# Gate z of the delta stage taken out of PSUM by halves during its last chunk, with the next products begun on the first half's bank, and a new order of VectorE's work at the turn

## The chip, the cores and the metric

One core of one Trainium2 chip. The metric is device microseconds of one execution. Before the change three runs gave a median of 2839.73 us (2836.88 to 2842.76).

## The reference, cut to what matters

Two transformer-like blocks on 256 tokens of width 2048, in float32. The change lies in the first mixer, a gated delta network with 32 value heads of 128:

```python
proj = h @ w_in
qkv, z, b, a = jnp.split(proj, [...], axis=-1)
qkv = jax.nn.silu(causal_depthwise_conv(qkv, conv_w))
q, k, v = ...                      # q and k scaled to length 1 per head
o = gated_delta_rule(q, k, v, g, beta)
o = o * lax.rsqrt(jnp.mean(o * o, -1, keepdims=True) + NORM_EPS)
o = (o.astype(h.dtype) * norm_w) * jax.nn.silu(z.reshape(B, S, GDN_V_HEADS, HEAD_DIM))
return o.reshape(B, S, GDN_DV) @ w_out
```

Here h is 256 x 2048 and w_in has 12352 columns. Behind this mixer come its output product, a layer norm, the feed-forward part and a second block; the change touches none of them.

## The kernel before, in words

The engines run as separate programs that meet at semaphores. Every matrix product is done in three fp32r products, high x high, high x low and low x high. A weight tile ("chunk") of 256 x 512 is loaded into `wr` (ring of 4); ScalarE copies it rounded to `wh` (`gh`, L1402 to L1406, ring of 3); GpSimd subtracts to get the rest `wl` (`low`, L594 to L598); TensorE multiplies. ScalarE may write the tile of chunk c once TensorE is through chunk c-3; GpSimd starts on it when ScalarE is through. In this document wl(n) is GpSimd's subtraction for chunk n of the next group and gh(n) ScalarE's copy for it.

The delta network is worked in 8 groups of 4 value heads (NIT = 8). A group takes 24 chunks: 8 for q and k (into PSUM tile `pg[0]`), 8 for v (`pg[1]`), 8 for z (`pg[0]` again). While the chunks of group j+1 run, the delta rule of group j is worked between them: TensorE runs one step of the generator `delta` behind nearly each chunk (`beside`, L1095 to L1110). The last step but one (rows "v1", "o1", "md1") stands ahead of chunk 23. The z chunks have tokens on the partitions: token half 0 goes to the first 512 columns of `pg[0]`, which is one PSUM bank, token half 1 to the second. In chunk 23 TensorE does the six products of half 0 first, then the six of half 1.

The **turn** is what lies between chunk 23 of one group and the first steps of the next:

- TensorE, chunk 0 of the next group (L797 to L831): waits for `s_zo` (z has left `pg[0]`), then 24 products. Behind it come step "ssq" of the next delta (L918; it waits for `s_sq1`, VectorE's squares of q and k, and for "md1", the end of VectorE's `mod_sum`, which reads the same PSUM tile), step "on" of the old one (eight transposes, L738), chunk 1, step "rows" (L926), chunk 2, step "gram" (L936; it waits for "qkn", VectorE's scaled q and k, L1948), and step "ktok", which waits for "dt" (VectorE, L1953).
- ScalarE: `gh(1)`, then the last step of the old delta: four squares with sums of the second half of the output (L1477), Ln and Exp for `rstd` (L1541, L1542), then `z_out` (L1452 to L1455: one copy of 128 x 1024 out of `pg[0]`), then `gh(2)`.
- VectorE: o1 (L2014), output times gate (L2018), `mod_sum` (a reduce out of PSUM, L2030, and a small addition, L2033), `squares` of q and k for the next group (L1913), output times `rstd` (L2025), and, once TensorE's transposes are done, `finish` (L2038). The next delta begins with four copies: L1942, and the three of `taps`, L1859, L1860 and L1861; then L1948 and L1953.
- GpSimd: wl(1), wl(2), then for the next group a product of 64 x 512 (L630), two DMA issues for the modulation weights (L591), wl(3), wl(4) and so on.

The product `mod_w` for the modulation vectors is done beside all this on VectorE (L1833, L1835). Six turns (groups 1 to 2 up to 6 to 7) have the z chunks of one group ahead of the q and k chunks of the next. The first turn has z in `pd[1]`, not in `pg[0]`. After the last group the output product (`ochunk`, L833 to L850) begins in place of chunk 0. On ScalarE and VectorE the iterations 0 to 5 are a hardware loop and iteration 6 stands behind it as straight code.

Of the kernel before, what the change touches and what calls it, by code (L numbers as in the profile page):

```python
# [17 lines left out]
ACT = mybir.ActivationFunctionType  # L18
# [8 lines left out]
NIT = NQK // 2  # L27
VH = 4
# [33 lines left out]
NCH = 24  # L62
N_GDN = NCH * (NIT + 1)
RING = 3
# [52 lines left out]
def build(nc, A, out):  # L117
    ctx = ExitStack()
    with ctx:
# [3 lines left out]
        def sem(name):  # L123
            return ctx.enter_context(nc.semaphore(name))
# [45 lines left out]
        zpend = take(VH, T)  # L170
# [167 lines left out]
        pg = [ctx.enter_context(nc.psum_tensor(f"pg{i}", [P, 1024], F32)) for i in range(2)]  # L338
        pd = [ctx.enter_context(nc.psum_tensor(f"pd{i}", [P, 1024], F32)) for i in range(2)]
# [17 lines left out]
        s_pk = sem("s_pk")  # L357
# [4 lines left out]
        s_qk = sem("s_qk")  # L362
        s_sq1 = sem("s_sq1")
        s_ot = sem("s_ot")
        s_zo = sem("s_zo")
        s_cv = sem("s_cv")
        s_acc = sem("s_acc")
# [367 lines left out]
        def _(pe):  # L735
# [30 lines left out]
            for t, n in enumerate(V_ROWS):  # L766
                dst = pd[0][:, 512 + t * P:512 + t * P + n] if t < 4 else pd[1][:, 512:512 + n]
                m = tr(dst, vstage[0:n, t, :])
# [4 lines left out]
            for kt in range(KD):  # L773
                b = kt // 4
# [4 lines left out]
                for t in range(TT):  # L779
                    m = tr((pg[0], pg[1], pd[1], pg[0])[b][:, (kt % 4) * T + t * P:(kt % 4) * T + (t + 1) * P],  # L780
                           xtok[:, t, kt * P:(kt + 1) * P])
# [13 lines left out]
            def gchunk(g, c):  # L795

                first_g = isinstance(g, int) and g == 0  # L797
                grp, kp = chunk_of(g, c)
                if c == 0 and not first_g:
                    pe.wait_ge(s_zo, g)  # L800
                    pe.wait_ge(s_cd, g * 2 - 1)
                if c == 8 and not first_g:
                    pe.wait_ge(s_cd, g * 2)
                if c == 16 and not first_g:
                    pe.wait_ge(s_cd, g * 2 + 1)
                pe.wait_ge(s_low, g * NCH + (c + 5))
                bank, first, last = pg[grp % 2], kp == 0, kp == 7
                if first_g and grp == 2:
                    bank = pd[1]
                if grp == 2:  # L810
                    for t in range(TT):
                        for k in range(2):
                            for i, (x, w) in enumerate(((0, wh), (0, wl), (1, wh))):
                                m = nc.tensor.matmul(halves(bank)[:, t, :], h_s[x][:, 2 * kp + k, t * P:(t + 1) * P],  # L814
                                                     w[c % RING][:, k, :], skip_group_check=True,
                                                     start=(first and k == 0 and i == 0),
                                                     stop=(last and k == 1 and i == 2))
                    m.then_inc(s_pk, 1)
                    return
                for n in range(4):  # L820
                    for k in range(2):
                        for i, (w, x) in enumerate(((wh, 0), (wh, 1), (wl, 0))):
                            m = nc.tensor.matmul(bank[:, n * T:(n + 1) * T], w[c % RING][:, k, n * P:(n + 1) * P],  # L823
                                                 h_s[x][:, 2 * kp + k, :], skip_group_check=True,
                                                 start=(first and k == 0 and i == 0 and n % 2 == 0),
                                                 stop=(last and k == 1 and i == 2))
                m.then_inc(s_pk, 1)

            def ochunk(c):

                if c == 0:  # L831
                    pe.wait_ge(s_zo, NIT)
                if c == 12:  # L833
                    pe.wait_ge(s_cd, NIT * 2)
                pe.wait_ge(s_low, NIT * NCH + (c + 5))
                g, kp = c // 12, c % 12
                if c == 0:
                    pe.wait_ge(s_osv, 1)
                elif 2 <= c < 12:
                    pe.wait_ge(s_os, kp // 2)  # L840
                for h in range(TT):
                    for k in range(2):
                        for i, (x, w) in enumerate(((0, wh), (0, wl), (1, wh))):
                            m = nc.tensor.matmul(halves(pg[g])[:, h, :], o_s[x][:, 2 * kp + k, h * P:(h + 1) * P],  # L844
                                                 w[c % RING][:, k, :], skip_group_check=True,
                                                 start=(kp == 0 and k == 0 and i == 0), stop=False)
                m.then_inc(s_pk, 1)
# [14 lines left out]
            for c in range(4):  # L862
                pe.wait_ge(s_h3, c + 1)
                m = gate_sums(c)
# [33 lines left out]
            for t, (row, w) in enumerate(((3, 0), (3, 1), (2, 0), (2, 1), (0, 0))):  # L898
                m = tr(pd[0][:, 512 + t * NH:512 + (t + 1) * NH], gx[0:NH, row, w * P:(w + 1) * P])
# [260 lines left out]
            for t in range(CK_FF):  # L1160
                g, k, last = out_chunk(t)
# [9 lines left out]
                if t == 4:  # L1171
                    pe.wait_ge(s_v, NIT * len(VO))
                    for i in range(2):
                        m = row_of(pd[i], 2 * KD + 8 * i)
                    m.then_inc(s_pp, 1)
                if t == 15:
# [4 lines left out]
                    for c in range(3):  # L1181
                        m = tr(pd[0][:, c * PAIRS:(c + 1) * PAIRS], araw[0:PAIRS, c, :])
                    m.then_inc(s_pp, 1)
                    for c in range(8):
                        m = tr(pd[1][:, c * P:(c + 1) * P], craw[1][:, c, :])
                    m.then_inc(s_pp, 1)
                if t == 19:
                    pe.wait_ge(s_craw[0], 128)
                    pe.wait_ge(s_ap, 2)
                    for c in range(8):  # L1190
                        m = tr(pd[0][:, c * P:(c + 1) * P], craw[0][:, c, :])
                    m.then_inc(s_pp, 1)
                if t == 38:
                    pe.wait_ge(s_vp, 1)
                    pe.wait_ge(s_ap, 4)
                    for i in range(2):
                        for c in range(8):
                            m = tr(pd[i][:, c * P:(c + 1) * P],
                                   bbar[i][:, 4 * c:4 * c + 4, :].rearrange("p a b -> p (a b)"))
# [150 lines left out]
        def _(act):  # L1350
            link, restart = chain(act, s_aa)
            a = nc.scalar.activation
# [96 lines left out]
                    a(pend[:, grp * 4 + n, :], pg[grp][:, n * T:(n + 1) * T], ACT.Copy,  # L1449
                      scale=cwc[:, 3, grp * 4 + n:grp * 4 + n + 1]).then_inc(s_cv, 1)  # L1450

            def z_out(g):  # L1452
                act.wait_ge(s_pk, g * NCH + (NCH + RING))
                a(zpend.rearrange("p a b -> p (a b)"), (pd[1] if isinstance(g, int) and g == 0 else pg[0])[:], ACT.Copy)\  # L1454
                    .then_inc(s_zo, 1)  # L1455

            def silu_qk(g):
# [7 lines left out]
                a(vT.rearrange("p a b -> p (a b)"), pend[:, 4:8, :].rearrange("p a b -> p (a b)"), ACT.Silu).then_inc(s_a, 1)  # L1465

            def silu_z(g):
                act.wait_ge(s_zo, g + 1)
                a(zt.rearrange("p a b -> p (a b)"), zpend.rearrange("p a b -> p (a b)"), ACT.Silu).then_inc(s_a, 1)

            def delta(it, more):
                bp, bv = it * len(PEO), it * len(VO)
                def PEw(name): act.wait_ge(s_pe, bp + PEO[name])
                def V(name): act.wait_ge(s_v, bv + VO[name])
                def squares(n0):
                    for n in range(n0, n0 + VH):
                        link(a(Tb[:, n, :], ob[:, n, :], ACT.Square, accum_out=ssq[:, n:n + 1]))  # L1477
                restart()
                PEw("ssq")
# [33 lines left out]
                for h in range(VH):  # L1513
                    m = a(vn0[:, h, :], pd[0][:, h * P:(h + 1) * P], ACT.Copy, scale=tkc[:, 2, h:h + 1])
# [6 lines left out]
                for h in range(VH):  # L1521
                    m = a(ob[:, VH + h, :], pd[0][:, 512 + h * P:512 + (h + 1) * P], ACT.Copy, scale=tkc[:, 4, h:h + 1])
# [5 lines left out]
                for h in range(VH):  # L1528
                    m = a(vn1[:, h, :], pd[1][:, h * P:(h + 1) * P], ACT.Copy, scale=tkc[:, 3, h:h + 1])
# [6 lines left out]
                    act.sem_inc(s_a, 1)  # L1536
                nc.scalar.preload_act_table_set("natural_log_exp_and_others")
                yield
                V("o1")
                squares(VH)  # L1540
                link(a(rstd, ssq, ACT.Ln, scale=1.0 / P, bias=cst[:, 0:1]))  # L1541
                a(rstd, rstd, ACT.Exp, scale=-0.5).then_inc(s_a, 1)  # L1542
                yield
# [11 lines left out]
            silu_qk(0)  # L1555
            gh(1, 0)
            gh(1, 1)
            z_out(0)
            gh(1, 2)
            silu_v(0)  # L1560
            nc.scalar.preload_act_table_set("natural_log_exp_and_others")
# [23 lines left out]

            def turn(j, more=None):

                z_out(j + 1)
                if more:
                    more()  # L1590
                gh(j + 2, 2)
# [197 lines left out]
        def _(dve):  # L1789
# [119 lines left out]
            def squares(it):  # L1909

                dve.wait_ge(s_qk, it + 1)
                fq = qk.rearrange("p a b -> p (a b)")
                v.tensor_tensor(sqb, fq, fq, ALU.mult).then_inc(s_sq1, 1)  # L1913
# [21 lines left out]
            def delta(it, mods):  # L1935
                bp, ba, bv = it * len(PEO), it * len(AO), it * len(VO)
                def PEw(name): dve.wait_ge(s_pe, bp + PEO[name])
                def Ac(name): dve.wait_ge(s_a, ba + AO0 + AO[name])
                def done(m): m.then_inc(s_v, 1)
# [10 lines left out]
                for c in range(TT):  # L1950
                    for h in range(VH):
                        n = c * VH + h
                        m = stt(out=dTb[:, n, :], in0=pd[0][:, n * P:(n + 1) * P], scalar=tkc[:, c, h:h + 1], in1=mneg[:],  # L1953
                                op0=ALU.subtract, op1=ALU.min)
# [4 lines left out]
                for c in range(TT):  # L1959
                    for h in range(VH):  # L1960
                        n, b = c * VH + h, c * 2 + h // 2
                        m = stt(out=lTb[:, n, :], in0=pd[1][:, b * P:(b + 1) * P], scalar=tkc[:, 2 + c, h:h + 1],
                                in1=dTb[:, n, :], op0=ALU.mult, op1=ALU.mult)
                done(m)
                dve.wait_ge(s_v, bv + VO["lt"])
                for b in range(2):
                    r = slice(64 * b, 64 * b + 64)
                    m = v.tensor_tensor(by_n(four(Uc[r])), heads(lTb[r, :, r]),
                                        m1t[r, 0:64].unsqueeze(1).unsqueeze(1).broadcast_to([64, 4, 2, 64]), ALU.mult)
# [46 lines left out]
                dve.wait_ge(s_v, bv + VO["o1"])  # L2016
                Ac("z")
                done(v.tensor_tensor(oz, ob, zt, ALU.mult))  # L2018
                PEw("md1")
                mod_sum(it, 1)  # L2020
                if mods:
                    squares(it + 1)
                dve.wait_ge(s_v, bv + VO["oz"])
                Ac("rstd")
                done(v.tensor_tensor(oz, oz, rstd.unsqueeze(2).broadcast_to([P, 8, P]), ALU.mult))  # L2025
# [295 lines left out]
            for t in range(TT):  # L2321
                for i in range(2):
                    part, cut = res[:, t, 1024 * i:1024 * (i + 1)], slice(1024 * i, 1024 * (i + 1))
# [169 lines left out]
```

## Time and profile before

| | |
|---|---|
| median of 3 runs | 2839.73 us (2836.88 to 2842.76) |
| the profiled execution's own time | 2838.75 us |
| its span, first to last instruction | 2836.8 us |
| TensorE busy | 2715.5 us (96%) |
| VectorE, ScalarE, GpSimd busy | 1948.6, 1208.2, 812.2 us |
| mean granted TensorE clock | 0.984 |

The span is 1.95 us shorter than the execution's time; that part lies around the program. All times of rows are us from the start of the span. A timeline row gives start, duration, engine, line, operation, operands and, in brackets, how long the engine had been idle and what ended it. Where a row joins several instructions the duration is that of all of them. An instruction whose start lies ahead of its predecessor's end is pipelined behind it.

### The profile page before, as it was taken

To read this page: it belongs to the slowest core of one execution; us is meant where nothing else is said; L and a number is where in the kernel's file an instruction comes from. 1 tells how busy PE (TensorE), PEld (TensorE's weight loads), DVE (VectorE), ACT (ScalarE), POOL (GpSimd) and SP (SyncE) were. 2 spreads that over 40 slices of the span, in tenths; PEclk is the share of its full clock that TensorE was granted. 3 is DMA by queue.
4 is the path that set the end of the run, shared out by engine and by line. 5 is a ranking of instruction groups with operands and counts; after the bars stand their busy time and mean duration, and the time that the engine had idled before them with its cause. 6 is when DMAs were issued, how large, how long until landed. Compare 5 with 4: busy or idle time off the path is not lost.

```text
span 2836.8 us, 48694 instructions
## 1 busy us (share of the span) xinstructions
PE 2715.5 (96%) x18902; PEld 2341.8 (83%) x18902; DVE 1948.6 (69%) x2285; ACT 1208.2 (43%) x1521; POOL 812.2 (29%) x554
## 2 busy tenths in 40 slices
PE   6999999999998999999999999969999999999998
PEld 3788988898896877888888888769999998888886
DVE  1377877787688667666666666685999899655554
ACT  2255455545545444433433333344333334543443
POOL 1066666676667510000000000000565562000000
PEclk8999999999999999999999999989999999999999
DMA  9866665675664666666666666535555555666664
GB/s 364 309 199 215 224 216 195 207 253 183 213 224 155 224 184 209 191 187 190 188 189 187 187 190 187 168 112 177 155 158 158 161 167 161 191 187 189 189 202 147
DMA packets 283912, 552.59 MB, mean 195 GB/s; under 512 B 16817, under 2 KB 54258, under 8 KB 282610
## 3 DMA queue, kind: packets, MB, share of 16 engines
q1 hardware_dynamic: 263632, 474.02, 54.3%
q0 software_dynamic: 19408, 76.06, 7.2%
q8 instruction: 122, 2.00, 0.3%
q10 hardware_dynamic: 722, 0.28, 0.0%
q14 instruction: 28, 0.23, 0.0%
HBM read 548.19 MB, written 2.10 MB: 194 GB/s over the span
## 4 chain that ended last, share of the span: by engine, by line
PE 80%; DVE 11%; ACT 4%; issue 2%; DMA 2%; DVEq 0%; POOL 0%; ACTq 0%; SPq 0%; POOLq 0%; PEld 0%
PE pg L1132 25%; PE pd L1132 17%; PE pg L823 13%; PE pg L1119 9%; PE pg L814 4%; DVE wl L2074 2%; PE pd L738 2%; PE pg L844 2%; DMA arena<-in_mod_w 1%; PE pd L987 1%; PE pd L1005 1%; DVE arena L2355 1%; DVE arena L2357 1%; DVE arena L2350 1%; ACT arena L1477 1%
## 5 line engine op out<-in xcount | busy, mean ns | idle before, releaser
L2074 DVE TENSOR_TENSOR wl<-wr,wh 128x1024 fp32r<-128x1024 f32 x616 | 773.7, 1265 | 507.7 <-ACT wh L1597 504.4
L1597 ACT ACTIVATE wh<-wr 128x1024 fp32r<-128x1024 f32 x616 | 652.7, 1060 | 997.7 <-PE pg L1132 405.4
L597 POOL TENSOR_TENSOR wl<-wr,wh 128x1024 fp32r<-128x1024 f32 x195 | 479.3, 2459 | 395.2 <-ACT wh L1406 395.0
L1406 ACT ACTIVATE wh<-wr 128x1024 fp32r<-128x1024 f32 x216 | 227.7, 1057 | 350.3 <-PE pg L823 219.9
L1119 PE MATMUL pg<-hh,wh 128*128 128x256 f32 x1280 | 366.5, 286 | 3.8 <-ACT arena L1715 2.5
L1119 PE MATMUL pg<-hl,wh 128*128 128x256 f32 x1280 | 363.0, 284 | 0.0
L1119 PE MATMUL pg<-hh,wl 128*128 128x256 f32 x1280 | 362.7, 283 | 0.0
L1132 PE MATMUL pg<-wh,hh 128*128 128x512 f32 x832 | 327.2, 393 | 0.0
L1132 PE MATMUL pg<-wl,hh 128*128 128x512 f32 x832 | 326.3, 392 | 0.0
L1132 PE MATMUL pg<-wh,hl 128*128 128x512 f32 x832 | 325.4, 391 | 0.0
L823 PE MATMUL pg<-hh,wh 128*128 128x256 f32 x1024 | 301.2, 294 | 14.8 <-ACT arena L1454 12.0
L1835 DVE SCALAR_TENSOR_TENSOR arena<-arena,condt 128x512 f32<-128x512 f32 x240 | 281.1, 1171 | 29.3 <-DMA arena<-in_mod_w 23.7
L823 PE MATMUL pg<-hl,wh 128*128 128x256 f32 x1024 | 290.2, 283 | 0.0
L823 PE MATMUL pg<-hh,wl 128*128 128x256 f32 x1024 | 290.0, 283 | 0.0
L1119 PEld LDWEIGHTS pg<-hh,wh 128*128 128x128 f32 x1280 | 246.1, 192 | 16.1 <-issue 13.4
L727 POOL COPY arena<-arena 128x256 f32 x8 | 6.4, 798 | 875.5 <-ACT arena L1715 875.5
L1119 PEld LDWEIGHTS pg<-hh,wl 128*128 128x128 f32 x1280 | 246.2, 192 | 0.0
L1119 PEld LDWEIGHTS pg<-hl,wh 128*128 128x128 f32 x1280 | 246.1, 192 | 0.0
L823 PEld LDWEIGHTS pg<-hh,wh 128*128 128x128 f32 x1024 | 196.4, 192 | 33.1 <-ACT arena L1454 14.6
L823 PEld LDWEIGHTS pg<-hl,wh 128*128 128x128 f32 x1024 | 196.8, 192 | 0.2 <-issue 0.2
L823 PEld LDWEIGHTS pg<-hh,wl 128*128 128x128 f32 x1024 | 196.7, 192 | 0.0
L1132 PEld LDWEIGHTS pg<-wh,hh 128*128 128x128 f32 x832 | 156.3, 188 | 34.9 <-issue 0.4
(392 smaller groups left out, 5033.1 us busy)
## 6 DMA issues: line engine op xcount, KB each, us to landing
wr<-in_w_in SPq DMA_DIRECT2D x224, 512.0 KB, 3.9
wr<-in_ffn_w_gu SPq DMA_DIRECT2D x176, 512.0 KB, 4.3
wr<-in_gdn_w_in SPq DMA_DIRECT2D x128, 512.0 KB, 4.0
arena<-in_mod_w POOLq DMA_DIRECT2D x64, 1024.0 KB, 7.4
wr<-in_ffn_w_down SPq DMA_DIRECT2D x88, 512.0 KB, 3.8
arena<-in_mod_w SPq DMA_DIRECT2D x32, 1024.0 KB, 12.2
wr<-in_gdn_w_in SPq DMA_DIRECT2D x128, 256.0 KB, 2.9
wr<-in_gdn_w_out SPq DMA_DIRECT2D x56, 512.0 KB, 4.7
```

Of the source, the lines that this page charges most:

```text
L597: nc.gpsimd.tensor_tensor(wl[c % RING][:], wraw[c % 4], wh[c % RING][:].bitcast(F32), ALU.subtract)\
L738: return nc.tensor.transpose(dst, src, ident[0:n, 0:n])
L814: m = nc.tensor.matmul(halves(bank)[:, t, :], h_s[x][:, 2 * kp + k, t * P:(t + 1) * P], w[c % RING][:, k, :], skip_group_check=True, start ...
L823: m = nc.tensor.matmul(bank[:, n * T:(n + 1) * T], w[c % RING][:, k, n * P:(n + 1) * P], h_s[x][:, 2 * kp + k, :], skip_group_check=True, ...
L844: m = nc.tensor.matmul(halves(pg[g])[:, h, :], o_s[x][:, 2 * kp + k, h * P:(h + 1) * P], w[c % RING][:, k, :], skip_group_check=True, star ...
L987: m = nc.tensor.matmul(block(pd[par], *crossed(s, b, n)), lTb[r, n, r], Tc[r, n, :], start=True, stop=True)
L1119: m = nc.tensor.matmul(bank[:, n * T:(n + 1) * T], w[s][:, k, n * P:(n + 1) * P], act[x][:, k0 + k, :], skip_group_check=True, start=(firs ...
L1132: m = nc.tensor.matmul(halves(bank)[:, h, :], act[x][:, k0 + k, h * P:(h + 1) * P], w[s][:, k, :], skip_group_check=True, start=(first and ...
L1406: a(wh[c % RING][:], wraw[c % 4], ACT.Copy).then_inc(s_hi, 1)
L1597: a(wh[c % 4][:], wraw[c % 4], ACT.Copy).then_inc(s_hc, 1)
L1835: m = stt(out=dst, in0=mw[t % 2][:, k, :], scalar=condt[:, kk:kk + 1], in1=dst, op0=ALU.mult, op1=ALU.add)
L2074: v.tensor_tensor(wl[c % 4][:], wraw[c % 4], wh[c % 4][:].bitcast(F32), ALU.subtract).then_inc(s_lc, 1)
```

## The change

z is taken out in two halves, each 512 columns. A new semaphore, `s_zh`, is raised by the last product of token half 0 in chunk 23; ScalarE's first half waits for it, the second half for the end of the chunk. The first half stands ahead of the four squares of the last delta step, the second between the second and the third of them. `s_zo` counts halves now. TensorE's chunk 0 waits for the first half ahead of its first 12 products and for the second half ahead of the other 12; the first chunk of the output product does the same by token halves. On VectorE `squares` of the next group stands ahead of `mod_sum` at the turn. In the first group both halves wait for the end of the chunk, one behind the other.

```diff
@@ gchunk (TensorE)
                 if c == 0 and not first_g:
-                    pe.wait_ge(s_zo, g)
                     pe.wait_ge(s_cd, g * 2 - 1)
...
+                        if last and t == 0 and not first_g:
+                            m.then_inc(s_zh, 1)
...
                 for n in range(4):
+                    if c == 0 and not first_g and n % 2 == 0:
+                        pe.wait_ge(s_zo, 2 * g - 1 + n // 2)
@@ ochunk (TensorE)
-                if c == 0:
-                    pe.wait_ge(s_zo, NIT)
...
                 for h in range(TT):
+                    if c == 0:
+                        pe.wait_ge(s_zo, 2 * NIT - 1 + h)
@@ ScalarE
-            def z_out(g):
-                act.wait_ge(s_pk, g * NCH + (NCH + RING))
-                a(zpend.rearrange("p a b -> p (a b)"), (pd[1] if isinstance(g, int) and g == 0 else pg[0])[:], ACT.Copy)\
+            def z_out(g, half):
+                first_g = isinstance(g, int) and g == 0
+                if half == 0 and not first_g:
+                    act.wait_ge(s_zh, g)
+                else:
+                    act.wait_ge(s_pk, g * NCH + (NCH + RING))
+                cut = slice(512 * half, 512 * half + 512)
+                a(zpend.rearrange("p a b -> p (a b)")[:, cut], (pd[1] if first_g else pg[0])[:, cut], ACT.Copy)\
                     .then_inc(s_zo, 1)
@@ delta (ScalarE), last step
                 yield
+                if more:
+                    z_out(it + 1, 0)
                 V("o1")
-                squares(VH)
+                squares(VH, 2)
+                if more:
+                    z_out(it + 1, 1)
+                squares(VH + 2, 2)
@@ turn (ScalarE)
-                z_out(j + 1)
@@ delta (VectorE), last step
                 done(v.tensor_tensor(oz, ob, zt, ALU.mult))
+                if mods:
+                    squares(it + 1)
                 PEw("md1")
                 mod_sum(it, 1)
-                if mods:
-                    squares(it + 1)
```

## Rows read from the trace of the kernel before

**Rows 1.** Waits of TensorE over the whole span: total us, times, longest.

```profile
PE pg L823 <- ACT arena L1454: 12.0, 6, 2.0
...
PE pd L918 <- DVE arena L1913: 2.4, 1, 2.4
```

**Rows 2.** Timeline of TensorE at the second of the six turns.

```profile
363.12 0.39 PE L814 MATMUL pg<-wh,hl 128*128 128x512 f32 x1
365.51 0.39 PE L823 MATMUL pg<-hh,wh 128*128 128x256 f32 x1 [2.00 <-ACT arena L1454]
...
368.48 1.88 PE L918 MATMUL pd<-arena,ones 128*128 128x512 f32 x4
```

**Rows 3.** Timeline of ScalarE at the same turn.

```profile
362.29 0.29 ACT L1477 ACTIVATE arena<-arena 128x128 f32<-128x128 f32 x1
...
364.46 1.01 ACT L1454 ACTIVATE arena<-pg 128x1024 f32<-128x1024 f32 x1
365.36 1.05 ACT L1406 ACTIVATE wh<-wr 128x1024 fp32r<-128x1024 f32 x1
```

**Rows 4.** Groups of ScalarE: busy us, mean ns, idle before.

```profile
L1490 ACT ACTIVATE arena<-pd 128x512 f32<-128x512 f32 x8 | 4.9, 614 | 0.0
```

**Rows 5.** Timeline of VectorE at the same turn.

```profile
362.38 0.69 DVE L2030 TENSOR_REDUCE arena<-pd 128x4 f32<-128x512 f32 x1
363.23 1.62 DVE L2033 TENSOR_TENSOR modt<-arena,vc 128x4 f32 x1 [0.16 <-DVE arena L2030]
364.77 1.21 DVE L1913 TENSOR_TENSOR arena<-arena 128x1024 f32<-128x1024 f32 x1
365.91 1.21 DVE L2025 TENSOR_TENSOR arena<-arena 128x1024 f32<-128x1024 f32 x1
371.38 1.28 DVE L2038 TENSOR_SCALAR arena<-pd,vc 128x1024 f32 x1 [4.26 <-PE pd L738]
...
372.93 1.38 DVE L1859 COPY arena<-vc 128x8 f32 x1 [0.18 <-DVE arena L1942]
...
374.91 1.22 DVE L1948 TENSOR_TENSOR arena<-arena 128x1024 f32<-128x1024 f32 x1
376.06 2.15 DVE L1953 SCALAR_TENSOR_TENSOR arena<-pd,arena,mneg 128x128 f32<-128x128 f32 x8
```

**Rows 6.** Timeline of GpSimd at the same turn.

```profile
362.46 2.37 POOL L597 TENSOR_TENSOR wl<-wr,wh 128x1024 fp32r<-128x1024 f32 x1 [2.89 <-ACT wh L1406]
366.49 2.87 POOL L597 TENSOR_TENSOR wl<-wr,wh 128x1024 fp32r<-128x1024 f32 x1 [1.66 <-ACT wh L1406]
...
370.30 1.54 POOL L591 DMA_DIRECT2D arena<-in_mod_w  x2
371.86 2.42 POOL L597 TENSOR_TENSOR wl<-wr,wh 128x1024 fp32r<-128x1024 f32 x1
375.27 3.13 POOL L597 TENSOR_TENSOR wl<-wr,wh 128x1024 fp32r<-128x1024 f32 x1 [0.99 <-ACT wh L1406]
```

**Rows 7.** The chain that ended last, same turn: start, us, what.

```profile
378.23 1.79 PE pd L936 x16
```

**Rows 8.** Timeline of VectorE and GpSimd at the start of the first delta iteration.

```profile
172.54 2.98 DVE L1860 COPY arena<-vc 128x8 f32 x1
...
171.48 1.58 POOL L591 DMA_DIRECT2D arena<-in_mod_w  x2
173.07 2.41 POOL L597 TENSOR_TENSOR wl<-wr,wh 128x1024 fp32r<-128x1024 f32 x1
```

**Rows 9.** Timeline of VectorE and GpSimd behind the last turn.

```profile
870.89 9.25 DVE L1948 TENSOR_TENSOR arena<-arena 128x1024 f32<-128x1024 f32 x1 [4.96 <-ACT arena L1482]
...
872.05 2.39 POOL L597 TENSOR_TENSOR wl<-wr,wh 128x1024 fp32r<-128x1024 f32 x1
```

**Rows 10.** Timeline of VectorE behind the sixth turn.

```profile
768.20 1.52 DVE L1859 COPY arena<-vc 128x8 f32<-128x8 f32 x1
769.76 0.17 DVE L1860 COPY arena<-vc 128x8 f32<-128x8 f32 x1
```

More of the change, by code:

```diff
@@ L364, in build @@
         s_ot = sem("s_ot")
+        s_zh = sem("s_zh")
         s_zo = sem("s_zo")
@@ L1467, in silu_z @@
             def silu_z(g):
-                act.wait_ge(s_zo, g + 1)
+                act.wait_ge(s_zo, 2 * g + 2)
                 a(zt.rearrange("p a b -> p (a b)"), zpend.rearrange("p a b -> p (a b)"), ACT.Silu).then_inc(s_a, 1)
@@ L1474, in V, with squares @@
                 def V(name): act.wait_ge(s_v, bv + VO[name])
-                def squares(n0):
-                    for n in range(n0, n0 + VH):
+                def squares(n0, count=VH):
+                    for n in range(n0, n0 + count):
                         link(a(Tb[:, n, :], ob[:, n, :], ACT.Square, accum_out=ssq[:, n:n + 1]))
@@ L1557, in _ @@
             gh(1, 1)
-            z_out(0)
+            z_out(0, 0)
+            z_out(0, 1)
             gh(1, 2)
```

## The prediction, made before the change was run

> **What bounds the kernel now.** I read the waits of TensorE first, since it is busy nearly all the time: only what it waits for is worth taking away. In all six turns chunk 0 stands 2.0 us until z has left PSUM, 12.0 us in all, and no other wait recurs in the loop; at the last turn TensorE waits instead for VectorE's squares [rows 1]. Then I laid the timelines of the four engines at one turn beside each other (the other five look the same). TensorE's last product of chunk 23 starts at 363.12, chunk 0 at 365.51, "ssq" at 368.48 [rows 2]. ScalarE is busy from 362.29 to 364.46 with squares, Ln and Exp before it takes z out [rows 3]. The reader should see in VectorE's and GpSimd's rows that some of their instructions exclude each other. The tiny addition L2033 takes 1.62 us and ends at 364.85, with wl(1), which ends at 364.83; the copy L1859 takes 1.38 us and ends at 374.31, with wl(3) at 374.28. The other way round, wl(2) takes 2.87 us and wl(4) 3.13 where others take 2.4, each behind a VectorE product (L2025, L1948) that had started first [rows 5, 6]. A VectorE instruction with PSUM input (L2030, L1953) isn't held. What counts at the turn is therefore also who asks first.
>
> **ScalarE's part.** A copy of 128 x 512 out of PSUM takes 0.61 us [rows 4] and, pipelined, moves its successor by about 0.5. z half 0 can start at 362.29: its products are done half a chunk ahead of the chunk's end, 363.51 (363.12 + 0.39), and some tenths of waiting would change nothing. It ends at 362.9. Two squares of 0.43 later (the 2.17 us from 362.29 to 364.46 hold four of them, Ln and Exp) half 1 starts at 363.65 and ends at 364.3. The two halves delay `rstd` by about 1.05 us, from 364.55 to 365.6; gh(2) starts at 365.5 in place of 365.36 [rows 3], as z_out no longer stands ahead of it.
>
> **TensorE's part.** The products are pipelined, so chunk 0 starts a little ahead of 363.51, at about 363.35; half 0 is out by then. Its 12 products on the first bank last 1.4 to 1.5 us (24 take 2.97 from 365.51 to 368.48), to 364.8, and half 1 is out at 364.3: no wait. That is 2.16 us earlier than 365.51; I take 2.2 us (the row of the wait says 2.0, which is the floor), or 13.2 for six turns. The two added waits in the chunk cost nothing while they are met, by 0.4 and 0.5 us. If they weren't, each would cost what ScalarE is late, with all of TensorE's queue behind it.
>
> **VectorE's part.** "ssq" now wants to start at 366.3. It needs the squares and the end of `mod_sum`, so the new order must deliver both. L1913 would start where L2030 does now, 362.38, and wl(1) asks at 362.46 [rows 5, 6]: VectorE is first by 0.08 us. The squares end at 363.6, wl(1) runs behind them until 365.85 (1.0 us later than now; chunk 1 needs it only behind "ssq" and "on", after 368), the reduce runs beside it, and L2033 is held until 365.87. "ssq" waits for nothing. L2025 follows at 365.8 (`rstd` is there), ends at 367.0, ahead of "on" at 368.0. So at chunk 0, "ssq" and "on" the whole 2.2 us is won.
>
> **Where it goes next.** All that TensorE releases comes 2.2 us earlier; GpSimd's chain doesn't. wl(2) begins behind L2025 as now, so the two DMA issues start at 370.16 and wl(3) at 371.72, 0.14 earlier than now. But gh(4) waits for TensorE's chunk 1, so wl(4), which now asks at 375.27 with 0.99 us of pause ahead of it [rows 6], could start at 373.1 and follows wl(3) at once. In that pause VectorE now does L1859's end, L1860, L1861 and the start of L1948, 0.36 us before wl(4) asks. After the change L2038 starts at 369.18, L1859 1.55 later at 370.73, and L1948 0.17 + 0.60 later [rows 5], at 371.5; the last copy, L1861, would start at 371.4. That is in the middle of the second DMA issue (370.93 to 371.70, half of 1.54 each). The first iteration shows a copy in that place: L1860, begun 0.27 us into the second issue, was held for 2.98 us, over the issue and the whole subtraction behind it [rows 8]. And where GpSimd runs instruction on instruction after its DMA issues, VectorE was not let in between: L1948 was held from 870.89 until 880.14, over the rest of one subtraction and three more [rows 9].
>
> By these rows L1861 is held until wl(4) ends, at 371.72 + 2 x 2.4 = 376.5. L1948 then ends at 377.65, "gram" starts at 377.7 (TensorE wants it at 376.0; today 378.23 [rows 7]), L1953 (2.15 us) ends at 379.75, and "ktok" starts at 379.8. Today "gram" ends at 378.23 + 1.79 = 380.02 and "ktok" starts there. So of 2.2 us per turn about 0.25 stay. The wait for z is gone, and "gram" and "ktok" wait in its place.
>
> The Trainium skill, page "SBUF — State Buffer", section "Who interferes with whom", gives as a rule that a VectorE instruction in a two-port mode or with two SBUF inputs and one of GpSimd exclude each other for the length of one instruction, and that issue order decides. The holds of L2033, L1859, wl(2) and wl(4) agree; the 9.25 us of L1948 over four instructions go further than the rule.
>
> **The sum.** Turns 1 to 5: 5 x 0.25 = 1.25 us. Behind the sixth turn the iteration is straight code and its copies follow each other faster: L1860 starts 1.56 us behind L1859, 0.04 behind its end [rows 10], so about 0.2 per copy in place of 0.33. L1861 would start about 0.35 earlier there, before the place in the second issue where L1860 was caught, and L1948 directly behind it: I take the full 2.2. The first turn has no wait for z; two copies in place of one add 0.15 to ScalarE, which then waits. At the last turn "ssq" waits for the squares; now it waits for `mod_sum`, the same work in another order. VectorE is first there too, and both orders end within 0.2 us: nothing (bounds 0.3 either way). Together 3.45 us. The profiled execution took 2838.75 (span 2836.8), which gives 2835.3 for it; against the median of 2839.73, 0.98 higher, 2836.2.
>
> The price that no row shows exactly is the hold at L1861. Its ends are no hold (2.2 us won per turn) and all three copies caught (below, 0.4 lost). I take the value in between since L1861's place is nearest to the copy of [rows 8].
>
> **Rivals.**
> - *A: the copies slip through.* If L1861 is let in at the end of the second DMA issue or isn't held at all, L1948 asks at about 371.5 to 371.8, together with wl(3) or ahead of it, and TensorE finds "qkn" ready. Six turns of 2.2 give 13.2: 2826.5. For it speak that L1861 is only 0.2 to 0.3 us from a free place and that no row shows L1861 itself held. Against it the copy of [rows 8].
> The Trainium skill's rule on page "SBUF — State Buffer", section "Who interferes with whom" (one instruction at a time), taken literally, lets VectorE in behind the second issue and stands for this case, 2826.5; [rows 9] speak against it.
> - *B: GpSimd is first at 362.46.* This is the case on the other side. The squares are then held until 364.83 and end at 365.95, the reduce at 366.65, and L2033 meets wl(2), asked for at 366.6: held until 369.0. "ssq" starts at 369.05 in place of 368.48, 0.55 later than today. Six turns lose 3.4: 2843.1. It decides if VectorE loses its 0.08 us. Against it: both starts are the same in all six turns.
> - *C: L1859 is caught in the first DMA issue.* Then all three copies follow wl(4): L1948 ends at 378.3, "ktok" starts at 380.4, 0.4 later than today; 2.5 lost, 2842.2.
> - *The change doesn't do what it says:* z isn't out in time. Only if half 1 came over 0.5 us late; no row suggests it.
>
> **How the numbers follow.** Forecast 0.45, A 0.30, B 0.08, C 0.09, and 0.08 for something unseen. About 0.2% (5.7 us) is what a measurement here can tell from no change. The likeliest case has its own range of 2832 to 2839.5: the floor of 2.0 per turn, the sixth turn either way, and the 3 us by which the three runs differ from their median. The range reaches from A to C, 2825 to 2842. Faster by over 0.2%: A, 0.10 of the forecast's and a little of the rest, 0.41. Slower by over 0.2%: the tails of B, C and the unseen, 0.09. Within: 0.50.
>
> **What would show it.** Right: no row of L823 waiting for L1454; L1913 at the turn straight behind L2018 with 1.2 us, wl(1) with about 3.4; wl(3) and wl(4) back to back; L1861 lasting some 5 us; L936 waiting for L1948 for about 1.7 us in five turns. Case A shows as L1948 ahead of wl(3) and turns that follow each other 2.2 us closer; B as L1913 lasting 3.5 us. I am wrong if TensorE waits at neither place and the time still doesn't fall, or if z half 1 is waited for.

## The result and the profile after

The changed kernel takes 2850.0 us (median of 7 runs, 2848.41 to 2856.32), the kernel before on the same chip 2841.52 (7 runs): a ratio of 1.0036, 95% interval [1.0025, 1.0047]. It is slower, by 0.36% as the ratio has it; the medians are 8.5 us apart. The prediction said 2836.2 with a range up to 2842.0, so it was wrong. The profiled execution is the slowest of the seven: 2856.32 us with a span of 2854.4, 17.6 longer than the span before. It is 6.3 us above the median, so part of what its rows show need not stand in the other six.

In this kernel the names have other lines: chunk 0 is L827 (was L823), ssq L922 (L918), rows L930 (L926), gram L940 (L936), ktok L739 (L738), the z copies L1463 (L1454), the three copies of `taps` L1873 to L1875 (L1859 to L1861), `squares` L1927 (L1913), scaled q and k L1962 (L1948), "dt" L1967 (L1953), GpSimd's subtraction L598 (L597), its DMA issue L592 (L591).

The waits of TensorE after, where [rows 1] had 12.0 us for z (us in total, times, longest):

```profile
PE pd L940 <- DVE arena L1962: 21.4, 7, 7.1
...
PE pd L739 <- DVE arena L2005: 5.0, 4, 2.1
PE pd L1009 <- DVE arena L2000: 4.4, 5, 1.1
...
PE pd L922 <- ACT arena L1444: 2.5, 1, 2.5
PE pd L922 <- DVE modt L2047: 2.3, 1, 2.3
...
PE pd L991 <- DVE arena L1992: 1.6, 3, 0.5
```

No row waits for z. "gram" waits for VectorE at all seven turns, once for 7.1 us. The wait of L922 for `mod_sum` (L2047) stands where [rows 1] had 2.4 us for the squares: the last turn's, the same work in another order, as forecast. The reader should then ask what VectorE did. ScalarE, VectorE and GpSimd at the second turn, the one of [rows 2 to 6]; everything stands 3.4 us later there, since TensorE's last product of chunk 23 begins at 366.49 in place of 363.12:

```profile
365.65 0.58 ACT L1463 ACTIVATE arena<-pg 128x512 f32<-128x512 f32 x1
...
367.06 0.60 ACT L1463 ACTIVATE arena<-pg 128x512 f32<-128x512 f32 x1
```

```profile
365.75 1.22 DVE L1927 TENSOR_TENSOR arena<-arena 128x1024 f32<-128x1024 f32 x1
366.88 0.69 DVE L2044 TENSOR_REDUCE arena<-pd 128x4 f32<-128x512 f32 x1
367.72 1.53 DVE L2047 TENSOR_TENSOR modt<-arena,vc 128x4 f32 x1 [0.16 <-DVE arena L2044]
...
372.49 1.28 DVE L2052 TENSOR_SCALAR arena<-pd,vc 128x1024 f32 x1 [2.10 <-PE pd L739]
373.69 0.17 DVE L1956 COPY arena<-arena 128x28 f32 x1
374.03 5.85 DVE L1873 COPY arena<-vc 128x8 f32 x1 [0.18 <-DVE arena L1956]
...
380.49 1.22 DVE L1962 TENSOR_TENSOR arena<-arena 128x1024 f32<-128x1024 f32 x1
```

```profile
365.82 3.41 POOL L598 TENSOR_TENSOR wl<-wr,wh 128x1024 fp32r<-128x1024 f32 x1 [2.89 <-ACT wh L1410]
...
372.58 1.03 POOL L631 TENSOR_TENSOR arena<-arena,masks 64x512 f32<-64x512 f32 x1
373.56 1.54 POOL L592 DMA_DIRECT2D arena<-in_mod_w  x2
375.12 4.73 POOL L598 TENSOR_TENSOR wl<-wr,wh 128x1024 fp32r<-128x1024 f32 x2
```

VectorE was first at 365.75, and wl(1) took 3.41 us, as forecast. Behind it wl(3) and wl(4) run back to back (4.73 us for two) where [rows 6] had a pause of 0.99. A copy of 128 x 8, begun 0.47 us into the first DMA issue, lasts 5.85 us: over the rest of that issue, the second one and both subtractions. In [rows 5] it took 1.38. Then TensorE, and below it the same place before:

```profile
366.49 0.39 PE L814 MATMUL pg<-wh,hl 128*128 128x512 f32 x1
...
381.76 2.05 PE L940 MATMUL pd<-arena 128*128 128x128 f32 x16 [2.44 <-DVE arena L1962]
383.84 0.87 PE L739 MATMUL pd<-ident,arena 128*128 128x128 f32 x6
```

```profile
378.06 1.95 PE L936 MATMUL pd<-arena 128*128 128x128 f32 x16
379.85 0.82 PE L738 MATMUL pd<-ident,arena 128*128 128x128 f32 x6
```

From the last product of chunk 23 it is 15.27 us to gram (381.76 - 366.49); before it was 14.94 (378.06 - 363.12). So the 2.0 us gained at chunk 0 and 0.3 more are gone by then.

**Where 17.6 us lie.** Gram starts at 182.46, 281.63, 381.76, 486.70, 586.85, 687.74, 788.11 and 896.73, before at 180.36, 279.22, 378.06 and on, 98.85 us apart, to 773.47, then 880.19. Six periods cost 12.5 us together, the last 1.9, the part behind it 1.1, and 2.1 are lost ahead of the first. These 2.1 come with the row of L922 waiting for ScalarE (L1444); the four products behind it take 3.45 us where they took 1.96 before, while the granted clock is at 0.50 for 3.4 us from 171.78 on. In four of the nine profiled kernels with the halves, this one among them, that wait was 2.5 us; in the other five and in the five without the halves it was 1.0 to 1.2. The same four, and no others, had the clock at 0.50 behind that wait. Why the wait differs stays open. Two of the periods are 100.1 us, 1.28 longer than before: 2.44 at gram, 0.54 at L991 and 0.29 in gram itself, from whose start it is 2.08 us to the next step (383.84 - 381.76) where it was 1.79 (379.85 - 378.06), against 2.0 for z. One period is 104.94: three waits at L1009 and two at L739, 4.2 us together, stand in it; whether the other executions have them isn't known. And at three of the gram waits the granted clock falls to the lower of its levels, 1.2 GHz, for 3.4 us each, from 588.21 and 789.59, behind the wait, and from 687.19, within it. The two periods into which the first two of these stretches fall, from 586.85 and from 687.74 on, are 100.89 and 100.37. The first stretch, where TensorE gets through 7 instructions in a microsecond in place of 10 (columns: stretch, us, busy time and instructions of PE, PEld, DVE, ACT and POOL, PEclk, DMA share, GB/s):

```profile
587.50:588.50 1.00, 1.00 (x10) 1.00 (x9) 1.00 (x5) 0.00 (x0) 0.00 (x0) 0.85 1.04 370
588.50:589.50 1.00, 1.00 (x7) 1.00 (x6) 0.96 (x4) 0.61 (x1) 0.00 (x0) 0.50 1.03 391
```

The same place before had 1.00 throughout (575.70 to 579.20). At the last turn the product that was held for 9.25 us in [rows 9] is held for more, this time from the start of the second of two DMA issues; VectorE and GpSimd there:

```profile
885.59 11.09 DVE L1962 TENSOR_TENSOR arena<-arena 128x1024 f32<-128x1024 f32 x1 [4.96 <-ACT arena L1491]
```

```profile
884.72 1.56 POOL L592 DMA_DIRECT2D arena<-in_mod_w  x2
886.30 2.40 POOL L651 TENSOR_TENSOR ol<-arena,oh 128x1024 fp32r<-128x1024 f32 x1
888.64 2.36 POOL L598 TENSOR_TENSOR wl<-wr,wh 128x1024 fp32r<-128x1024 f32 x1
890.96 2.33 POOL L651 TENSOR_TENSOR ol<-arena,oh 128x1024 fp32r<-128x1024 f32 x1
893.26 2.33 POOL L598 TENSOR_TENSOR wl<-wr,wh 128x1024 fp32r<-128x1024 f32 x1
```

### The profile page after: what moved, and what is told of

It is laid out like the page before. It is cut to its first block, busy times and chain, and to the rows that moved or that the text cites. A ratio compares the mean times of both kernels' runs of the same rounds, so it can differ in the third digit from the quotient of the medians.

```text
span 2854.4 us, 48709 instructions
## 1 busy us (share of the span) xinstructions
PE 2721.9 (95%) x18902; PEld 2348.2 (82%) x18902; DVE 1989.6 (70%) x2285; ACT 1207.6 (42%) x1529; POOL 814.4 (29%) x554
## 4 chain that ended last, share of the span: by engine, by line
PE 77%; DVE 15%; DMA 3%; issue 3%; ACT 2%; POOL 1%; DVEq 0%; ACTq 0%; SPq 0%; POOLq 0%; PEld 0%
PE pg L1136 25%; PE pd L1136 17%; PE pg L827 10%; PE pg L1123 9%; PE pg L814 5%; DMA arena<-in_mod_w 2%; DVE wl L2088 2%; PE pd L739 2%; DVE arena L1849 2%; DVE arena L1873 1%; DVE arena L2369 1%; DVE arena L2371 1%; DVE arena L2364 1%; PE pd L991 1%; PE pd L1009 1%
## 5 line engine op out<-in xcount | busy, mean ns | idle before, releaser
L598 POOL TENSOR_TENSOR wl<-wr,wh 128x1024 fp32r<-128x1024 f32 x195 | 481.3, 2471 | 401.7 <-ACT wh L1410 401.5
L1849 DVE SCALAR_TENSOR_TENSOR arena<-arena,condt 128x512 f32<-128x512 f32 x240 | 287.6, 1198 | 26.6 <-DMA arena<-in_mod_w 21.1
L827 PE MATMUL pg<-hh,wh 128*128 128x256 f32 x1024 | 300.8, 294 | 2.7 <-POOL wl L598 2.7
L827 PE MATMUL pg<-hl,wh 128*128 128x256 f32 x1024 | 290.2, 283 | 0.0
L827 PE MATMUL pg<-hh,wl 128*128 128x256 f32 x1024 | 289.9, 283 | 0.0
L827 PEld LDWEIGHTS pg<-hh,wh 128*128 128x128 f32 x1024 | 196.9, 192 | 19.0 <-issue 13.6
L827 PEld LDWEIGHTS pg<-hl,wh 128*128 128x128 f32 x1024 | 196.9, 192 | 0.5 <-issue 0.3
L827 PEld LDWEIGHTS pg<-hh,wl 128*128 128x128 f32 x1024 | 196.6, 192 | 0.0
```

The lines of the kernel that those rows point to most:

```text
L598: nc.gpsimd.tensor_tensor(wl[c % RING][:], wraw[c % 4], wh[c % RING][:].bitcast(F32), ALU.subtract)\
L1849: m = stt(out=dst, in0=mw[t % 2][:, k, :], scalar=condt[:, kk:kk + 1], in1=dst, op0=ALU.mult, op1=ALU.add)
```

## The experiments

Ratios are to the kernel before on the same chip. Runs named together shared a chip, so their times can be compared directly.

**1. Which half of the change does it.** First kernel, the halves with VectorE's old order:

```diff
                 done(v.tensor_tensor(oz, ob, zt, ALU.mult))
-                if mods:
-                    squares(it + 1)
                 PEw("md1")
                 mod_sum(it, 1)
+                if mods:
+                    squares(it + 1)
```

> Halves of z as in the changed kernel, VectorE's order at the turn as before (mod_sum ahead of squares). Theory T (the three copies of taps are held behind GpSimd's DMA issues and the two subtractions that now follow without a pause, and this alone eats the 2.2 us of each turn and more): the order matters little, 2847 to 2853 us, L1873-type copy held for over 5 us in the loop. Rival R1 (the new order on VectorE, which delays the first subtraction by 1 us, is what costs): the gain of the halves shows, 2828 to 2832 us.

Measured: 2849.49 us, ratio 1.0039 [1.0025, 1.0053]. Second, the new order alone, in the kernel before:

> VectorE's order alone, z in one piece behind the last squares as before. T: z is still waited for 2.0 us per turn, GpSimd keeps its pause, nothing moves: 2838 to 2844 us. R1: the order costs, 2848 us or more.

Measured: 2838.52 us, ratio 0.9995 [0.9986, 1.0005]. VectorE's order is worth nothing either way; the loss belongs to the halves. In the first kernel gram waits in the same place (waits of TensorE):

```profile
PE pd L940 <- DVE arena L1962: 22.0, 7, 6.9
```

**2. Is it the copies?** Third and fourth kernel: the three copies of `taps` moved from the head of an iteration into the middle of the one before, behind VectorE's products for "rhs1" (those of the first iteration ahead of it); once in the changed kernel, once in the one before.

```diff
@@ delta (VectorE), head
-                if mods:
-                    done(taps(it + 1))
-                else:
-                    dve.sem_inc(s_v, 1)
+                dve.sem_inc(s_v, 1)
...
                 done(m)
+                if tap_next:
+                    link(taps(it + 2))
                 yield
```

> The changed kernel with the three copies of taps moved from the start of the delta iteration to the end of the one before (behind rhs1, where VectorE then idles about 7 us). T: VectorE's scaled q and k are ready before GpSimd's third subtraction, TensorE waits at neither place, turns 2.2 us closer than before: 2826 to 2831 us, loop period 96.7 us. R2 (TensorE would have stood somewhere else anyway, as at the weights, so that the wait for z was never worth anything): 2840 us or more.

> The kernel before with only the three copies moved. T and R2: VectorE had 2.1 us of slack at this place, so nothing: 2838 to 2844 us, period 98.85. If the copies themselves were on the path, it would be 1 us per turn or more faster, 2835 or less.

Measured: 2842.69 us, ratio 1.0013 [1.0004, 1.0023], and 2839.1, ratio 0.9997 [0.9987, 1.0007]. The first missed its forecast by 12 us and lies in the range of R2; but experiment 3 gets the 2.2 us per turn back, which R2 rules out. The miss has another reason; VectorE and GpSimd:

```profile
373.46 6.84 DVE L1960 TENSOR_TENSOR arena<-arena 128x1024 f32<-128x1024 f32 x1 [0.24 <-ACT arena L1491]
```

```profile
372.92 1.54 POOL L592 DMA_DIRECT2D arena<-in_mod_w  x2
374.48 4.73 POOL L598 TENSOR_TENSOR wl<-wr,wh 128x1024 fp32r<-128x1024 f32 x2
```

The product (L1960 there) that asked 0.54 us into the first issue is caught as the copy was, until wl(4) ends at 379.21. The copies weren't the cause, they only stood first in the queue.

**3. Take GpSimd's DMA issues away from the turn.** The first two loads of modulation weights of each iteration are issued in the iteration before, behind wl(0) of the group after next (those of the first iteration ahead of the loop):

```diff
@@ batch (GpSimd)
-                for t in range(2):
-                    mod_load(it * 8 + 32, t)
...
                         low(it + 2, t)
+                        if t == 0:
+                            mod_load(it * 8 + 40, 0)
+                            mod_load(it * 8 + 40, 1)
```

In the kernel before:

> The kernel before with GpSimd's first two DMA issues of each delta iteration moved ahead, behind the first subtraction of the next group's ring (where GpSimd idles about 3 us). Theory T2: a run of GpSimd instructions that begins with DMA issues doesn't let a waiting VectorE instruction in, one without them does. Then in the loop nothing changes (slack), and behind the last turn, where L1948 was held 9.25 us behind such a run, it is held 2.5 us at most: 2833 to 2837 us. Rival U (any run of back-to-back GpSimd instructions shuts VectorE out, whatever it begins with): L1948 is still held 5 to 9 us there: 2838 to 2842 us.

In the changed one, alone, with the copies moved too, and the latter with VectorE's old order:

> The changed kernel with the same two DMA issues moved ahead. T2: the copies and the scaled q and k are held for one subtraction at most; TensorE waits at gram for 0 to 1 us in place of 2.4: 2824 to 2833 us. U: the subtractions 3 and 4 still follow each other, and the copies are still held over both: 2845 us or more.

> The changed kernel with the DMA issues and the three copies moved. T2: nothing is late at gram, the loop's period is 96.6 to 96.8 us, the last turn gains too: 2820 to 2828 us. U: the scaled q and k are held over two subtractions, 2838 us or more.

> As the run before, with VectorE's order at the turn as in the kernel before. T2: squares are done at the same time as chunk 0, so within 2 us of it, 2820 to 2830 us. If the order is what makes it possible to start ssq early, it is 5 us or more slower than that run.

Measured, in this order: 2838.53 us, ratio 0.9991 [0.9981, 1.0001]; 2832.35, ratio 0.997 [0.9957, 0.9982]; 2823.87, ratio 0.9933 [0.9917, 0.995]; 2823.77, ratio 0.9938 [0.9921, 0.9954]. In the second of them VectorE gets in twice at the turn; VectorE, then GpSimd:

```profile
370.35 1.96 DVE L1876 COPY arena<-vc 128x8 f32 x1 [0.18 <-DVE arena L1959]
372.45 0.17 DVE L1877 COPY arena<-vc 128x8 f32 x1
372.78 2.33 DVE L1878 COPY arena<-vc 128x16 f32 x1 [0.15 <-DVE arena L1877]
375.02 1.21 DVE L1965 TENSOR_TENSOR arena<-arena 128x1024 f32<-128x1024 f32 x1
```

```profile
369.89 2.39 POOL L598 TENSOR_TENSOR wl<-wr,wh 128x1024 fp32r<-128x1024 f32 x1
372.68 2.40 POOL L598 TENSOR_TENSOR wl<-wr,wh 128x1024 fp32r<-128x1024 f32 x1 [0.41 <-ACT wh L1413]
```

Between wl(3) and wl(4) there is now a pause of 0.41 us, in which one copy slips through and the next is caught. With the copies away the product itself takes that pause, and no turn of the loop has a wait. The chain that ended last, of the third kernel (L943 is gram):

```profile
278.97 1.79 PE pd L943 x16
375.55 1.79 PE pd L943 x16
472.14 1.79 PE pd L943 x16
```

The period is 96.59 us, 2.26 shorter than the 98.85 of before: what the halves of z were to bring. Neither move is worth anything in the kernel before (ratios 0.9997 and 0.9991). Both together were run with the halves only; that they would be worth nothing without them, as gram has no wait in the loop before, is argued.

The kernel before with the loads moved also settles a question of mechanism. I had supposed that it takes a DMA issue to shut VectorE out for several instructions. At its last turn there is none near; VectorE and GpSimd:

```profile
870.86 7.73 DVE L1951 TENSOR_TENSOR arena<-arena 128x1024 f32<-128x1024 f32 x1 [4.95 <-ACT arena L1485]
```

```profile
865.80 4.73 POOL L651 TENSOR_TENSOR ol<-arena,oh 128x1024 fp32r<-128x1024 f32 x2
870.48 2.38 POOL L597 TENSOR_TENSOR wl<-wr,wh 128x1024 fp32r<-128x1024 f32 x1
872.83 2.38 POOL L651 TENSOR_TENSOR ol<-arena,oh 128x1024 fp32r<-128x1024 f32 x1
875.17 2.33 POOL L597 TENSOR_TENSOR wl<-wr,wh 128x1024 fp32r<-128x1024 f32 x1
```

The product is held over the rest of one subtraction and two more, to their end at 877.5. An unbroken run of GpSimd instructions is enough.

**4. Give VectorE a pause on purpose.** GpSimd waits for "qkn", VectorE's scaled q and k, ahead of wl(3) of each iteration: in the changed kernel, in the best one so far, and in the kernel before.

```diff
@@ batch (GpSimd)
                         o_low(t + 1)
+                    if t == 1:
+                        pool.wait_ge(s_v, it * len(VO) + VO["qkn"])
                     low(it + 1, t + 2)
```

> The changed kernel and nothing else than one wait: GpSimd waits for VectorE's scaled q and k (L1948 of before) ahead of its third subtraction, so that it pauses there. Theory T3, from the runs so far: a waiting VectorE instruction is let in behind a GpSimd instruction only if that one began behind a pause or was itself held. The pause ends the hold: copies below 1.5 us, TensorE doesn't wait at gram in the loop, and behind the last turn it waits 5 us less: 2820 to 2827 us. Rival H (the halves and the earlier chunk 0 cost elsewhere what they win): 2836 us or more.

> The changed kernel with the DMA issues and the copies moved, and the same wait. T3: the loop is as without the wait (nothing was late there), and behind the last turn the scaled q and k are no longer held for four subtractions (TensorE waited 5.5 us at gram): 4 to 5 us faster than without the wait, 2818 to 2821 us. H': GpSimd, now later, becomes what TensorE waits for in the last group: no gain, 2822 us or more.

> The kernel before with the wait alone. T3: nothing in the loop, and 4 to 5 us behind the last turn, where TensorE waited 5.2 us at gram: 2834 to 2837 us. If the wait costs in the loop, 2842 us or more.

Measured: 2830.88 us, ratio 0.997 [0.9958, 0.9983]; 2827.95, ratio 0.996 [0.9946, 0.9974]; 2844.16, ratio 1.0018 [1.0009, 1.0027]. One semaphore wait, with nothing moved, turns the change from 0.36% slower to 0.3% faster, so it is GpSimd's run that costs it. VectorE and GpSimd at the second turn of the first of them:

```profile
371.81 0.28 DVE L1875 COPY arena<-vc 128x8 f32 x1 [0.18 <-DVE arena L1958]
...
372.70 1.23 DVE L1964 TENSOR_TENSOR arena<-arena 128x1024 f32<-128x1024 f32 x1
```

```profile
371.33 1.54 POOL L592 DMA_DIRECT2D arena<-in_mod_w  x2
374.11 7.08 POOL L598 TENSOR_TENSOR wl<-wr,wh 128x1024 fp32r<-128x1024 f32 x3 [1.24 <-ACT wh L1412]
```

The first copy asks 0.48 us into the first issue, where it was caught in the changed kernel (0.47), and is through in 0.28; the product, asked for in the second issue, isn't held at all. What differs is the pause of 1.24 us behind the issues. So it is the subtractions straight behind the issues that make the hold long, and not the issues alone.

All three end 4 to 7 us above their forecasts, the second and third in the range of their rivals (2822 or more, 2842 or more): the work that GpSimd puts off comes later. In the output product TensorE waits 5.0, 5.6 and 5.1 us for GpSimd's subtractions, 1.9 in the best kernel and 2.2 before. TensorE's waits in the delta rule, and VectorE 20 us behind the turn, of the first of them:

```profile
PE pd L974 <- DVE arena L1984: 7.8, 6, 1.3
```

```profile
384.66 4.75 DVE L1984 TENSOR_TENSOR arena<-arena,m1t 64x512 f32<-64x512 f32 x2
```

These two products took 1.44 us in the best kernel. The subtractions that come late now stand against them, and behind each of the six turns there is a wait of 1.3 us; the period is 97.96.

At the last turn the wait was worth 4.8 us (period 100.58 against 105.37). So the last kernel has it in that iteration alone, on top of the best kernel (`if t == 1 and o_low:`):

> This is the fastest kernel so far (halves of z, GpSimd's two DMA issues moved ahead, the three copies moved away; 2823.87 us, ratio 0.9933) with GpSimd's wait for VectorE's scaled q and k only in the last iteration, where VectorE's product is held for 9.54 us and gram waits 5.49 us. In the kernel that had this wait in every iteration the last period was 100.58 us in place of 105.37, each period of the loop 97.96 in place of 96.59, and the time behind the last gram was 2.4 us longer, since GpSimd's subtractions then came late for the output product. Theory (the wait costs 1.37 us in each turn of the loop and gives 4.8 less 2.4 at the last turn): loop periods 96.59, last period about 100.6, 2.4 us faster than 2823.87, so about 2821.5 and a ratio of 0.9925. Rival (what the wait gives at the last turn comes back whole from GpSimd's late subtractions): 2824 to 2825, ratio 0.9933 or above.

Measured: 2819.52 us (2819.32 to 2822.36), ratio 0.9932 [0.9919, 0.9946]. Its five first periods are 96.59 and the last is 101.36, 4.0 less than in the best kernel, but the sixth is 99.06, with a wait of 2.0 us at L1054 that the best kernel doesn't have. The ratio is that of the best kernel, 0.9933 [0.9917, 0.995], measured in other runs: the two can't be told apart, and the question between theory and rival stays open. Both beat the kernel before by about 0.7%.

## Why the prediction was wrong, by its own steps

- **ScalarE, TensorE, VectorE at the turn: right.** z leaves in 0.58 and 0.60 us, chunk 0 follows chunk 23 without a wait, the squares start 0.07 us ahead of wl(1) and take 1.22, wl(1) 3.41. The 2.2 us per turn are real: the two kernels in which TensorE waits for nothing in the loop have 2.26.
- **Where it goes next: right in kind.** wl(3) and wl(4) back to back, the gain turned into a wait at gram. The wait was put at 1.7 us and measured at 2.4.
- **The step that failed is the place of the hold.** L1861 was to be caught in the second issue. It was the first copy, L1859, in the first issue: rival C, given 0.09. The forecast had that copy start at 370.73, which is 0.57 us into an issue that begins at 370.16; it measured 0.47 into it. The prediction gives no reason for letting it pass. In the first iteration of the kernel before a copy 0.74 us into the first issue, of 0.82 us, does pass, but no row of a place like this one stood behind it. The runs fill the gap: asks 0.33, 0.47 and 0.54 us into the first issue are all caught where the two subtractions follow at once, and one 0.48 us into it isn't where a pause follows. The hold thus stood ahead of all three copies, and the other two came behind it: 0.33 us each, most of the 0.7 by which the wait at gram is longer than forecast.
- **The size of C: right at the turn, short behind it.** C put "ktok" 0.4 us later than before. Measured from chunk 23's last product it is 0.62 (383.84 - 366.49 = 17.35 against 379.85 - 363.12 = 16.73; the prediction's 380.02 is the end of gram, not the start of "ktok"). But the period grows by 1.28 and more. C's sum ended where TensorE has its operands at "ktok"; VectorE was still late for L991, L1009 and L739, and the clock fell at three of the waits. No such cost was in the sum, and the range ended at C, 2842.2, where 2850.0 was measured.
- **The sixth turn: wrong.** It was to keep the full 2.2 us, and gram waited 2.16 there too. VectorE and GpSimd at that turn of the changed kernel:

```profile
780.51 5.99 DVE L1873 COPY arena<-vc 128x8 f32<-128x8 f32 x1
```

```profile
780.18 1.54 POOL L592 DMA_DIRECT2D arena<-in_mod_w  x2
```

  The first copy came 0.33 us into the first issue. In the straight code the ask comes 0.14 us earlier in the issue than in the loop (0.47), and is caught all the same.
- **The last turn: wrong.** It was put at nothing, with bounds of 0.3. Its period is 1.9 us longer, since the product came within the second of GpSimd's DMA issues and not behind them.
- **Rival A** (2826.5 if nothing is held) was a true price of the halves: the kernels with GpSimd's issues moved and the copies away measure 2823.87, and 6 x 2.26 = 13.6 us of that are the loop's. **Rival B** never came about: the squares take 1.22 us at every turn.

The Trainium skill, page "SBUF — State Buffer", section "Who interferes with whom", would have VectorE and GpSimd exclude each other for the length of one instruction. The rows of the changed kernel, 5.85 us to the end of the second subtraction and 11.09 over four, go further, and the measurement decides.

## What to carry to other kernels

When a wait of the bounding engine is taken away, lay the timelines of the other engines beside each other as they will stand then, and look for pauses that close: VectorE may live on a pause of GpSimd. An ask that falls inside a GpSimd run with subtractions in it should be taken as held to the end of the run, to the next pause, also where a neighbouring row shows a pass, and its lateness followed for several steps, not to the first. The cure was to move GpSimd's issues and VectorE's small copies out of the place where the two meet; alone each was worth nothing in the old kernel.

## What was unexpected of the hardware

I counted, in the delta stage of all fourteen traces, the ends of GpSimd's products and subtractions at which a VectorE instruction without PSUM operands was waiting and another GpSimd instruction was next. Where the GpSimd instruction had begun behind a pause, or had itself been held, VectorE was let in every time, in over 500 cases (how many depends on how much lateness counts as waiting). Where it had begun straight behind another GpSimd instruction and ran at its usual length, VectorE was not let in 65 times out of 73. These are the same few places of the program, again in each turn and each kernel, so they are fewer than 73 independent cases. This is read from traces; what decides it in the hardware, and the eight exceptions, stay open. That one pause of 0.41 us let a copy in, and one semaphore wait changed the time by 0.7%, speaks for it.

A DMA issue of GpSimd (0.77 us) by itself holds VectorE little: an instruction without PSUM operands asked within a single issue, with a pause behind it, was held for 0.33 us at most, in some 700 cases. With subtractions straight behind the issues a copy, and also a product of 128 x 1024 with both inputs in SBUF, asked 0.54 us into the first, is held to their end. Not always: in the first iteration of the kernels with the copies moved alone, a copy asked about 0.26 us into the first issue was through in 0.52 and 0.54 us, ahead of the second issue and the subtraction.

In the changed kernel an idle TensorE of 2.4 us (2.2 at the sixth turn) went with 3.4 us at 0.50 of the clock in three of the six turns (586.85, 687.74 and 788.11), and with none in the other three.
